# Expert results added onto the residual in SBUF by one-hot products, in place of a scatter to memory and a reload

## The reference

```
x = x + gt1 * mixer_output(...)
h2 = modulate(rmsnorm(x, g_norm2), sh2, sc2)
x = x + gt2 * hier_moe(h2, ...)
y = rmsnorm(x, g_final)
```

## Time and profile before

| what | value |
|---|---|
| median of 3 runs | 2027.92 us (2025.12 to 2039.0) |
| the profiled execution, its own time | 2026.33 us |
| its span, first to last instruction | 2024.7 us |
| the turns' loop, first gate product to last down product | 531.4 us (1448.4 to 1979.8) |
| what follows the loop | 44.9 us |
| mean granted clock of PE | 0.928 of full speed |
| mean rate of the DMA engines | 269 GB/s over the span |

### The profile page before, as it was taken

The page is one execution under the profiler, slowest core; times in us unless marked ns, Lnnn a source line. Parts: engine busy times, 40 slices in busy tenths (PEclk is TensorE's granted clock), DMA queues, the critical chain, the costliest instruction groups (busy, mean ns, idle before and its releaser), DMA issues.

```text
span 2024.7 us, 26921 instructions
## 1 busy us (share of the span) xinstructions
PE 1723.5 (85%) x10776; PEld 1089.3 (54%) x10776; DVE 461.8 (23%) x834; ACT 200.4 (10%) x399; POOL 170.2 (8%) x304
## 2 busy tenths in 40 slices
PE   7589999999998999999576999998888787788771
PEld 3156666666666777777454777775533232333230
DVE  2020000000017643333666211002311010101015
ACT  2010000000001110111223110001400000000001
POOL 1011021111110000150000000000000000000000
PEclk9789999999999999999888999998898888888895
DMA  9997586775705432652899983323499999999993
GB/s 361 419 357 281 218 291 235 264 269 189 268 22 178 148 102 99 193 165 87 322 410 410 369 319 136 126 102 148 161 394 404 401 404 398 415 394 409 394 364 150
DMA packets 146153, 545.53 MB, mean 269 GB/s; under 512 B 18005, under 2 KB 55035, under 8 KB 118539
## 3 DMA queue, kind: packets, MB, share of 16 engines
q1 hardware_dynamic: 118724, 439.53, 56.3%
q0 software_dynamic: 19088, 104.88, 14.5%
q10 hardware_dynamic: 8288, 0.39, 0.3%
HBM read 517.23 MB, written 27.53 MB: 269 GB/s over the span
## 4 chain that ended last, share of the span: by engine, by line
PE 57%; DMA 29%; DVE 6%; issue 4%; SPq 3%; DVEq 1%; ACT 1%; POOLq 0%; POOL 0%; ACTq 0%
PE ps L626 56%; DMA ring<-in_w_up_e_dram 19%; DMA xT<-in_w_ada_dram 4%; DMA ring<-in_cache_k_dram 3%; DMA ring<-in_w_ada_dram 2%; PE ps L636 2%; SPq L375 1%; DVE ring L1690 1%; DVE ring L1334 1%; SPq L381 1%; DVE ring L1340 1%; DMA z<-in_x_sample_dram 0%; DVE z L1343 0%; DVE ring L1430 0%; DMA ring<-y_rows 0%
## 5 line engine op out<-in xcount | busy, mean ns | idle before, releaser
L626 PE MATMUL ps<-hT,ring 128*128 128x288 f32 x2560 | 650.4, 412 | 8.3 <-ACT hT L1168 6.4
L626 PEld LDWEIGHTS ps<-hT,ring 128*128 128x128 f32 x2560 | 484.3, 192 | 179.2 <-issue 51.1
L626 PE MATMUL ps<-ring,work 128*64 128x512 f32 (+1 forms) x1280 | 297.9, 683 | 101.5 <-DMA ring<-in_w_up_e_dram 77.3
L626 PE MATMUL ps<-ring,z 32*32 32x256 f32 (+3 forms) x3744 | 229.9, 449 | 67.6 <-DVE ring L1690 54.8
L1343 DVE COPY z<-ps 128x256 f32<-128x256 f32 (+6 forms) x98 | 64.4, 660 | 947.3 <-PE ps L626 906.8
L626 PE MATMUL ps<-z,ring 128*128 128x288 f32 (+1 forms) x1040 | 256.0, 407 | 5.7 <-PE ps L626 3.0
L626 PEld LDWEIGHTS ps<-ring,work 128*64 128x64 f32 (+1 forms) x1280 | 99.7, 146 | 297.2 <-issue 259.8
L626 PEld LDWEIGHTS ps<-z,ring 128*128 128x128 f32 x1040 | 196.5, 190 | 63.4 <-issue 8.0
L626 PEld LDWEIGHTS ps<-ring,z 32*32 32x32 f32 (+3 forms) x3744 | 114.0, 122 | 171.5 <-issue 164.3
L1168 ACT ACTIVATE z<-ps 128x512 f32<-128x512 f32 (+5 forms) x104 | 50.0, 539 | 948.8 <-PE ps L626 929.2
L636 PE MATMUL ps<-ident,z 64*128 64x64 f32 (+4 forms) x644 | 91.4, 286 | 29.1 <-DVE z L1334 9.8
(11 more groups left out here) (203 smaller groups left out, 723.4 us busy)
## 6 DMA issues: line engine op xcount, KB each, us to landing
ring<-in_w_in_dram SPq DMA_DIRECT2D x40, 2048.0 KB, 12.4
xT<-in_w_ada_dram POOLq DMA_DIRECT2D x64, 1024.0 KB, 7.4
ring<-in_w_gate_e_dram SPq DMA_DIRECT2D x32, 2048.0 KB, 18.2
ring<-in_w_up_e_dram SPq DMA_DIRECT2D x32, 2048.0 KB, 24.4
ring<-in_w_down_e_dram SPq DMA_DIRECT2D x32, 2048.0 KB, 22.8
ring<-in_w_ada_dram SPq DMA_DIRECT2D x16, 2048.0 KB, 26.0
ring<-in_cache_k_dram SPq DMA_DIRECT2D x64, 512.0 KB, 6.7
ring<-in_cache_v_dram SPq DMA_DIRECT2D x64, 512.0 KB, 7.6
```

Of the source, the lines that this page charges most:

```text
L626: return nc.tensor.matmul(o, lhsT, rhs, start=start, stop=stop, skip_group_check=free)
```

## The change

Nothing goes to memory and back any more. Each turn builds `spots`, a table of 128 slots by 288 tokens that holds a slot's weight at its token's column and zero elsewhere. The results in `y_out` are multiplied by it: `combine(turn, n)` does, for one of 3 chunks of 96 tokens and one half of the columns, two products of 64 rows by 96 columns into banks 6 and 7 (one for each half of the width). `add_pair(turn, n)` on DVE multiplies the 96 x 1024 result by the gate and adds it to the residual, which is now kept as `x3`, 96 tokens on partitions by 3 chunks. A turn has 6 of these pairs. Those of a turn's results run in the next turn, after the steps k = 1, 3 and 6 of each half of the gate and up products; those of the last turn run after the loop. In the first turn `spots` and `y_out` hold zeros. The weight is no longer multiplied into `hid`. The list has 2 numbers for each slot where it had 3. The sample rows' gates are spread to 96 columns after the list is ready. The chunks at the end are 3 of 96 tokens, all added up before the first is normalized.

```diff
@@ GpSimd, its loop
                 pool.wait_ge(sem("hs_turned"), it + 2)
                 gather(it + 2)
-                pool.wait_ge(sem("y_copied"), it + 1)
-                pool.tensor_copy(put, listed_i[:, ds(2 * it + 1, 1)])
-                pool.drain()
-                pool.indirect_dma_start(y_rows, bass.IndirectOffsetOnAxis(ap=put, axis=0), y_out, None).then_inc(sem("y_put"), 16)
-                pool.wait_ge(sem("y_put"), 16 * it + 16)
-                pool.sem_inc(sem("y_out_free"), 1)
@@ TensorE
+            def combine(turn, n):
+
+                c, j = n // 2, n % 2
+                if n == 0:
+                    pe.wait_ge(sem("y_copied"), turn + 1)
+                pe.wait_ge(sem("combined_read"), turn * 6 + (n + 1))
+                for u in range(2):
+                    rows = slice(u * W, (u + 1) * W)
+                    last = mm(ps[0:TT, 6 + u, :], spots[rows, c * TT:(c + 1) * TT], y_out[rows, j * 512:(j + 1) * 512], True, True)
+                last.then_inc(sem("combined"), 1)
...
                             last = mm(ps[u * W:(u + 1) * W, 0, :], hs[:, half * 8 + k, :], w, half == 0 and k == 0, half == 1 and k == 7)
                             if k == 7:
                                 last.then_inc(sem(f"ring_free{(MOE + n) % SLOTS}"), 1)
+                        if k in (1, 3, 6):
+                            combine(it, 3 * half + (1, 3, 6).index(k))
...
+            for n in range(6):
+                combine(windows, n)
@@ VectorE
+            def add_pair(turn, n):
+
+                c, j = n // 2, n % 2
+                cols = [a.rearrange("p (u j n) -> p u j n", u=2, j=2)[:, :, j] for a in (x3[:, c, :], gate_s if c == NT - 1 else gate_p)]
+                v.wait_ge(sem("combined"), turn * 6 + (n + 1))
+                tt(gated, ps[0:TT, 6:8, :], cols[1], ALU.mult)
+                v.drain()
+                v.sem_inc(sem("combined_read"), 1)
+                tt(cols[0], cols[0], gated, ALU.add)
+                v.drain()
...
             with v.Fori(0, windows) as it:
+                for n in range(6):
+                    add_pair(it, n)
                 v.wait_ge(*used(MOE + 3, it))
                 copy(up_s, ps[W:2 * W, 0, :])
...
-                stt(hid, sg, weight[0:W, ds(it, 1)], up_s, ALU.mult, ALU.mult).then_inc(sem("hid_ready"), 1)
+                tt(hid, sg, up_s, ALU.mult).then_inc(sem("hid_ready"), 1)
+                copy(now, listed[:, ds(it, 1), :].rearrange("p w n -> p (w n)"))
+                v.drain()
+                tsc(spots, iota_pos, now[:, 0:1], now[:, 1:2], ALU.is_equal, ALU.mult)
...
-                v.wait_ge(sem("y_out_free"), it + 1)
@@ VectorE, after the loop
+            for n in range(6):
+                add_pair(windows, n)
+                if n % 2:
+                    v.sem_inc(sem("x3_ready"), 1)
             v.wait_ge(sem("gf_loaded"), 16)
...
+            for c in range(NT):
+                finish(c)
```

More of the change, by code:

```diff
@@ L242, in build @@
         wrt = work2[:, 2480:2480 + KT * 20].rearrange("p (k n) -> p k n", n=20)
[L243 to L251, removed]
+        entry = work2[0:TT, 2800:2800 + NT * 4].rearrange("p (i n) -> p i n", n=2)
+        listing = work2[0:TT, 512:512 + NT * 2 * NWIN * 2].rearrange("p (i w n) -> p i w n", w=NWIN, n=2)
+        gate_p = hflat[0:TT, 0:D]
+        gate_s = hflat[0:TT, D:2 * D]
+        listed = ms[:, 0:2 * NWIN].rearrange("p (w n) -> p w n", n=2)
+        now = ms[:, 2 * NWIN:2 * NWIN + 2]
+        token_i = rstd[0:W, 0:NWIN].bitcast(I32)
         take = rstd[0:W, 64:65].bitcast(I32)
-        put = rstd[:, 65:66].bitcast(I32)
+        spots = xflat[:, 1024:1024 + T]
+        gated = xflat[0:TT, 2048:2048 + 1024].rearrange("p (u n) -> p u n", u=2)
+        x3_sq = ring[0:TT, 0:D]
         tok_ss = xflat[:, 200:203]
         tok_rs = xflat[:, 204:207]
-        gate_exp = work2[:, 0:KT * TS].rearrange("p (k t) -> p k t", t=TS)
+        gate_exp = xflat[:, 2048:2048 + KT * TT].rearrange("p (k t) -> p k t", t=TT)
         gf_row = z[:, 0:D]
@@ L448, in _ @@
                 expert(e, w + 1)
[L450 to L456, removed]
-                sp.wait_ge(sem("out_ready"), c + 1)
[L458 to L462, removed]
+            for c in range(NT):
+                sp.wait_ge(sem("out_ready"), c + 1)
+                n = min(TT, TP - c * TT)
+                sp.dma_start(out["y_prompt"][0, c * TT:c * TT + n, :], x3[0:n, c, :]).then_inc(sem("y_stored"), 16)
+            sp.dma_start(out["y_sample"].rearrange("b t n -> (b t) n"), x3[TT - TS:TT, NT - 1, :]).then_inc(sem("y_stored"), 16)
+            sp.wait_ge(sem("y_stored"), (NT + 1) * 16)
         @block.gpsimd
@@ L581, in _ @@
                                pattern=[[1, TT]], channel_multiplier=-1)
[L582 to L584 removed]
+            pool.iota(entry.rearrange("p (c s) n -> p c s n", s=2)[:, :, :, 0], pattern=[[TT, NT], [0, 2]], base=0,
+                      channel_multiplier=1, allow_small_or_imprecise_dtypes=True)
             pool.iota(slot_no, pattern=[[0, 2], [1, W]], base=0, channel_multiplier=0, allow_small_or_imprecise_dtypes=True)
[L586 to L590 removed]
             pool.drain()
@@ L596, in gather @@
             def gather(w):
-                pool.tensor_copy(take, listed_i[0:W, ds(2 * w, 1)])
+                pool.tensor_copy(take, token_i[:, ds(w, 1)])
                 pool.drain()
@@ L1111, in _ @@
                     k = 4 * (n % 4) + m
[L1112 to L1115, removed]
+                    gate = modT[:, 5 * KT + k, 0:1].to_broadcast([P, TT]) if n < 4 else gate_exp[:, k, :]
+                    last = tr(ps[0:TT, 2 + n % 4, m * P:(m + 1) * P], gate)
                 last.then_inc(sem("gate_turned"), 1)
@@ L1909, in _ @@
             v.drain()
-            for n in range(3):
+            for n in range(2):
                 tt(listing[:, :, :, n], in_turn, entry[:, :, n:n + 1].to_broadcast([TT, 6, NWIN]), ALU.mult)
```

76 lines of the change are left out of this document (29 added, 47 removed).

## The result

The changed kernel takes **2049.7 us** (median of 8 runs, 2047.2 to 2053.2) against 2027.3 for the one before: a ratio of 1.0108, with a 95% interval from 1.0086 to 1.0129. The forecast was 2049.

What follows compares the result with a forecast made beforehand. The loop was taken as bound by the weights' transfer, and by PE after the change. Span: 2024.7 + 33.6 (loop) - 11.1 (tail) - 1.0 (ahead of it) = 2046.2 us; forecast 2049, 8 in 10 range 2010 to 2090.

Steps and rivals of the forecast that it cites:

- PE takes over from the transfers: Turns' loop: PE's turn of 35.3 us exceeds the 32.2 the transfers need, so PE becomes the bound.
- The turn: One turn of the loop: 24.7 + 6.9 + 1.6 + 2.1 = 35.3 us.
- insertion: Two products on PE, taken as parallel, plus array shape changes: 1.15 us each, six per turn, 6.9 us.
- delay of the hidden rows: Sixth pair on DVE precedes the up result's copy, so PE waits 1.6 us longer per turn; bounds 1.3 to 2.0.
- The clock term: Down products after PE's light stretch lose 2.1 us per turn to half clock; bounds 0 and 2.8.
- The first turn: Turn 0 of the loop: 27.0 + 8.5 = 35.5 us.
- The tail: After the loop: six pairs, normalizations and stores take 33.8 us against 44.9, 11.1 us less.
- what is ahead of the loop: List product, list and casts before the loop get shorter: 1.0 us less, bounds 0 and 1.5.
- PE bound, at full clock: Rival for the loop: PE keeps its clock, turn 33.2 us, time 2018 us; chance 0.2.
- One after the other: Rival: an insertion's two products don't run at once, 0.85 us more each, 2136 us in all; chance 0.1.
- Dearer insertions: Rival: shape changes cost 0.7 us each time round, insertion 1.55, 38 us over the forecast, 2087; chance 0.12.
- Still bound by the transfers: Rival for the loop: PE needs 32.0 us, transfers hold the turn at 32.2, time about 2003; chance 0.08.

Runs made afterwards that it cites:

- e1: Changed kernel with a scatter of the 128 result rows, read by nobody, put back into every turn, and DVE's wait for it: 2050.3 us.
- e3: Changed kernel with only three of the six pairs done per turn, the other columns getting no expert result: 1989.8 us.
- e8: Changed kernel with no insertion or pair in the loop; only the last turn's results are added, after it: 2001.8 us.
- e5: Changed kernel with four useless products per turn between the transposes and PE's wait for the hidden product: 2019.2 us.
- e2: Changed kernel with both products of each insertion reading partitions 0 to 63, so they share rows of the array: 2155.2 us.
- e4: Changed kernel with the second half's three insertions after steps 0, 2 and 4 in place of 1, 3 and 6: 2009.9 us.
- e7: Changed kernel with e6's edit; tail pairs alternate between two sets of PSUM banks, first chunk normalized after the fourth pair: 2003.9 us.
- e6: Changed kernel with the sixth insertion moved between transposes and the hidden-product wait, its pair on DVE after the turned hidden rows' copy: 2007.9 us.

## Why the prediction was right

- **PE takes over from the transfers.** Shown by e1 (more transfer, same time), by the missing waits, and by e3 and e8 (with fewer insertions the transfers bind again).
- **The turn.** Forecast 35.3 us; measured 35.3. Its terms: insertion 1.15, measured 1.17 on average, so 7.0 us for six where 6.9 was forecast; all parts at full clock 33.2, measured 33.26 in e5; delay of the hidden rows 1.6, measured 2.16 - 0.6 = 1.6; clock 2.1, measured 2.0. The clock term had the least ground, a place between a mean and a worst case; that it came out is partly luck, and e2 (2.6) and e4 (0.9) show how it moves with what precedes. The first turn was forecast without a clock term, at 35.5 us, and took 37.5, with 8.78 us of down products; the loop is 1.6 us over the forecast, mainly for it.
- **The tail and what is ahead of the loop.** 33.8 forecast, 34.1 measured, but by two errors that cancel. The six pairs took 19.3 us, not 21.1, because PE kept its full clock for three of them; and from the last vector operation to the end it was 5.5 us (2042.8 to 2048.3), not 3.4. For what is ahead of the loop 1.0 was forecast and 0.8 measured, which confirms nothing: the start of the loop lies between 1442.7 (e7) and 1456.3 (e8) in kernels that are the same up to there.
- **The whole.** The span was forecast at 2046.2 and is 2048.3, 2.1 us over. The time comes within 1 us of 2049 because the forecast added 1.6 us for the place of one profiled execution among its runs, and the changed kernel's profiled execution, at 2050.1, was no faster than its median. The agreement is better than the method. The prediction took 1% as what a measurement can tell from no change; the interval of the ratio is 0.4% wide, so the 1.1% is clear.
- **The rivals.** "PE bound, at full clock" was put at 2018; e5, which makes just that case, took 2019. "One after the other" was put at 2136 and took 2155 in e2: the clock and the tail at half clock were undersized. "Dearer insertions" is excluded by the mean of 1.17. Its price was also not what its own reason gives: the dearer 0.45 for both changes would be 0.9 and not 0.7, an insertion of 1.75 and a kernel 58 us over the forecast, not 38. "Still bound by the transfers" is not what the change does, but what e6 makes of it, at 2008 and not 2003, since the limit was set some 0.5 us too low.

## What to carry to other kernels

Work that is moved from an engine or a queue that is the bound is only a gain up to the room of the engine that takes it: write down that engine's full turn (here 24.7 us), add the insertions, the waits that they cause further down and the clock that it will lose, and compare with the bound. Then look at where the insertions stand: the same six cost 40 us more when the last one delays a chain (after against e4, where three of them stand elsewhere), and one of them costs 0.16 us where it fills a wait (e6). A gap on TensorE costs twice once TensorE is the bound, in itself and in the clock of what follows (1.6 and 2.0 us per turn here).

## What was not expected

Useless products in a wait of 2.2 us brought the granted clock of 14 turns from 0.93 to 1.00 and took 30 us off the kernel, and the turn became the same to 0.01 us. With the gap cut from 2.16 to 0.48 us (e4), the first ten turns alternated strictly between 31.58 and 33.28 us, one with a stretch at half clock in it and one without. The changed kernel has such a pattern too: three turns of 34.96, 34.75 and 36.10 us, with down products of 8.8, 8.5 and 9.9 us, come round again and again to the end of the loop.
